# Expert weights in 4 MB loads of 32 KB per partition, and a new order at the end of the expert stage

## What is computed

```python
logits = h @ router_w + router_b
top_logit, top_e = lax.top_k(logits, 4)            # 4 of 32 experts for each token
gate = jnp.minimum(xe @ w_gate[e] + b_gate[e], 7.0)
up = jnp.clip(xe @ w_up[e] + b_up[e], -7.0, 7.0)
act = (up + 1) * (gate * jax.nn.sigmoid(1.702 * gate))
y = act @ w_down[e] + b_down[e]                     # times the token's weight, summed over its experts
```

## Time and profile before

| | |
|---|---|
| median of the runs | 1764.72 us |
| the profiled execution's own time | 1764.61 us |
| its span, first to last instruction | 1762.8 us |
| PE busy | 1638.9 us, 93% |
| DVE busy | 731.0 us, 41% |
| ACT busy | 283.2 us, 16% |
| granted PE clock, mean | 0.992 of full speed |
| moved by DMA | 537.21 MB |
| mean DMA rate | 305 GB/s |

### The profile page before, as it was taken

One profiled execution on the slowest core, in us unless ns is written; L12 is line 12 of the kernel. 1 busy time (PEld: TensorE's weight loads), 2 busy tenths in 40 slices (PEclk: granted clock), 3 DMA queues, 4 the chain that ended last, 5 costly groups with the idle time before them and its releaser, 6 DMA issues.

```text
span 1762.8 us, 19011 instructions
## 1 busy us (share of the span) xinstructions
PE 1638.9 (93%) x7248; PEld 887.6 (50%) x7248; DVE 731.0 (41%) x1325; ACT 283.2 (16%) x623; POOL 25.2 (1%) x30
## 2 busy tenths in 40 slices
PE   5999999999999798898997988998999999999998
PEld 3466686534333242332332423332686878888743
DVE  3785532332324223233142232332234663777755
ACT  3123450301010010100100101000243334010000
POOL 0110000000000000000000000000000000000000
PEclk9999999999999999999999999999999999999999
DMA  9895235899999999999999999999624333444440
GB/s 381 299 332 163 96 111 204 342 430 429 431 430 429 430 430 430 429 430 430 430 429 430 429 430 430 430 429 418 220 96 143 129 111 144 143 173 162 153 181 24
DMA packets 86255, 537.21 MB, mean 305 GB/s; under 512 B 6160, under 2 KB 7568, under 8 KB 59952
## 3 DMA queue, kind: packets, MB, share of 16 engines
q1 hardware_dynamic: 82384, 530.60, 74.2%
q10 hardware_dynamic: 3808, 5.78, 0.9%
HBM read 535.31 MB, written 1.05 MB: 304 GB/s over the span
## 4 chain that ended last, share of the span: by engine, by line
PE 69%; DMA 24%; DVE 4%; DVEq 1%; issue 1%; ACT 1%; POOL 0%; ACTq 0%; SPq 0%
PE ps L1953 22%; PE ps L2332 22%; DMA ring<-in_w_up 12%; DMA ring<-in_w_gate 10%; PE ps L2678 6%; PE ps L2872 5%; PE ps L2308 3%; PE ps L2393 2%; DMA arena<-in_w_down 2%; PE ps L2783 1%; DVE arena L1163 1%; DMA const<-in_const 1%; PE ps L2189 1%; PE ps L1965 1%; PE ps L2372 0%
## 5 line engine op out<-in xcount | busy, mean ns | idle before, releaser
L2332 PE MATMUL ps<-ring,arena 128*64 128x512 f32 x2288 | 513.8, 597 | 54.0 <-DMA ring<-in_w_gate 21.0
L2332 PEld LDWEIGHTS ps<-ring,arena 128*64 128x64 f32 x2288 | 161.2, 137 | 388.0 <-issue 316.7
L1953 PE MATMUL ps<-arena,ring 128*128 128x256 f32 x896 | 199.9, 381 | 0.3 <-ACT arena L790 0.3
L2332 PE MATMUL ps<-arena 128*64 128x512 f32 x784 | 177.8, 598 | 12.1 <-DMA arena<-in_w_up 5.7
L1953 PEld LDWEIGHTS ps<-arena,ring 128*128 128x128 f32 x896 | 168.4, 190 | 33.2 <-issue 6.8
L1953 PE MATMUL ps<-ring,arena 128*128 128x512 f32 (+1 forms) x480 | 164.0, 496 | 1.5 <-ACT arena L907 1.3
L862 ACT ACTIVATE arena<-ps 128x512 f32<-128x512 f32 x32 | 19.1, 598 | 670.4 <-PE ps L2372 670.4
L1953 PEld LDWEIGHTS ps<-ring,arena 128*128 128x128 f32 x480 | 90.8, 191 | 65.0 <-issue 56.9
L2332 PEld LDWEIGHTS ps<-arena 128*64 128x64 f32 x784 | 55.5, 138 | 120.2 <-issue 103.6
L1448 DVE TENSOR_TENSOR arena<-ps,arena 128x512 f32<-128x512 f32 x32 | 22.1, 692 | 201.2 <-PE ps L2332 201.2
L1473 DVE TENSOR_TENSOR arena<-ps,g_moe 64x512 f32<-64x512 f32 x32 | 21.9, 684 | 189.5 <-PE ps L2332 189.5
(11 more groups left out here) (351 smaller groups left out, 1558.5 us busy)
## 6 DMA issues: line engine op xcount, KB each, us to landing
ring<-in_w_up SPq DMA_DIRECT2D x54, 2048.0 KB, 33.8
ring<-in_w_down SPq DMA_DIRECT2D x54, 2048.0 KB, 32.2
ring<-in_w_gate SPq DMA_DIRECT2D x47, 2048.0 KB, 33.6
ring<-in_w_in SPq DMA_DIRECT2D x23, 2048.0 KB, 8.1
arena<-in_w_down SPq DMA_DIRECT2D x17, 2048.0 KB, 32.0
arena<-in_w_up SPq DMA_DIRECT2D x16, 2048.0 KB, 31.3
arena<-in_w_gate SPq DMA_DIRECT2D x15, 2048.0 KB, 30.8
ring<-in_w_ada SPq DMA_DIRECT2D x12, 2048.0 KB, 17.1
```

Of the source, the lines that this page charges most:

```text
L1953: last = pe.matmul(dst, a, b, start=k == 0, stop=k == len(terms) - 1)
L2332: mm = pe.matmul(dst[CAP * g:CAP * g + CAP, :], stationary(half, c), w[:, c, 512 * g:512 * g + 512], start=half == 0 and c == 0, stop=half ...
```

## The change

A matrix is read eight rows to a partition: partition p holds rows 8p to 8p + 7, 32 KB in one piece, in one load of 4 MB into two adjacent slots (slots 5 and 6 are now in `arena`). Such a load waits until both slots are free, and PE waits for it before the first half. This holds from block 18 of the first group to block 19 of the last, 170 blocks in 85 loads. Blocks 0 to 17 of the first group, down 2 and down 3 of the last come as halves of 2 MB (four of a partition's eight rows, 16 KB), and the last half in four loads, one matrix row of each partition (4 KB) at a time. The first blocks go out in the order 4, 6, 7, 5, 8.

Feature 8p + c now stands on partition p. The gate and up products take as moving operand, for each half of the bank, groups of four columns out of every eight (`by_rows`), so that what follows keeps its layout. The biases are loaded in whole rows and put in that order by two copies on POOL, whose buffer lies where `hperm` is written later, so ACT waits for them before its first copy. The shift comes by eight matmuls of 64 columns for each of n = 6 and n = 7. The first gather waits for all four copies to `hperm`.

In the last group the branch comes after gate 3 and the turn of expert 2's activation. Behind it stand up 3, all four rows of the first combine, down 2, the turn of expert 3's activation, down 3, and the second combine, whose first row waits for the first half of `y_out` alone.

```diff
-        hperm = area(1024, 2048).rearrange("p (t h c d) -> p t h c d", t=TT, h=2, c=4)
+        hperm = area(1024, 2048).rearrange("p (t j d) -> p t j d", t=TT, j=KC)
+        btab_in = area(1024, 2048)
...
+        PAIRED = 18
...
+        def moe_area(s, slots=1):
+
+            r = moe_ring(s)
+            return area(13312 + SLOT * (s - 5), SLOT * slots) if r is None else ring[:, r * SLOT:(r + slots) * SLOT]
+
+        def moe_block(k):
+            a = area(7680, SLOT) if k == ASIDE else moe_area(moe_place(k) % MRING)
+            return a.rearrange("p (c n) -> p c n", c=4)
+
+        def moe_pair(k):
+            return moe_area(moe_place(k) % MRING, 2)
+
         def moe_ring(s):
 
-            return None if s in (4, 5) else (W_MOE + (s if s < 4 else s - 2)) % RING
-
-        def moe_block(k):
-            if k == ASIDE:
-                return area(7680, SLOT).rearrange("p (c n) -> p c n", c=4)
-            s = moe_place(k) % MRING
-            r = moe_ring(s)
-            a = ring[:, r * SLOT:(r + 1) * SLOT] if r is not None else area(13312 + SLOT * (s - 4), SLOT)
-            return a.rearrange("p (c n) -> p c n", c=4)
+            return None if s in (5, 6) else (W_MOE + (s if s < 5 else s - 2)) % RING
...
+        PAIRED_AT = (1, 3, 5, 7)
+        LAST_BLOCK = N_EXP * BLK_EXP - 1
+        HALF_LOADS = [k for k in range(PAIRED) if k != ASIDE] + [LAST_BLOCK - 2, LAST_BLOCK]
+        LAST_HALVES = ((EG - 2, 2), (EG - 1, 2))
...
+            def matrix(g, q, m):
+                return t[("w_gate", "w_up", "w_down")[m]][bass.ds(g * EG + q, 1), :, :].rearrange(
+                    "e (p c) n -> p (e c) n", c=KC)
+
             def block_load(X, g, q, m, half, k):
-                src = t[("w_gate", "w_up", "w_down")[m]][bass.ds(g * EG + q, 1), half * 512:half * 512 + 512, :]
-                sp_.dma_start(moe_block(k).rearrange("p c n -> p (c n)"),
-                              src.rearrange("e (p c) n -> p (e c n)", c=4)).then_inc(moe_loaded(k), 16)
-
-            def expert_load(X, u, g, q, m, last=False):
+                sp_.dma_start(moe_block(k), matrix(g, q, m)[:, 4 * half:4 * half + 4, :]).then_inc(moe_loaded(k), 16)
+
+            def expert_load(X, u, g, q, m, last, start):
 
                 k = weight_block(q, m, last)
-                for half in range(2):
-                    sp_.wait_ge(X["used"], u * GROUP_BLOCKS + (X["before"] - MRING + k + half + 1))
-                    block_load(X, g, q, m, half, k + half)
-
-            def group_loads(X, u, g, last, done=0):
...
+                order = {4: (1, 0), 6: (1, 1), 8: (0, 2), 10: (2, 0), 12: (2, 1)}
+                for n in (4, 6, 7, 5, 8, 9, 10, 11, 12, 13) if first else range(4, 14):
+                    (q, m), half = order[n - n % 2], n % 2
+                    if not first:
+                        sp_.wait_ge(X["used"], u * GROUP_BLOCKS + (X["before"] - MRING + n + 1))
+                    elif n == 6:
+                        sp_.wait_ge(sem("merged_done"), 4)
+                    elif n in (4, 5, 8):
+                        sp_.wait_ge(X["used"], W_MOE - RING + {4: 4, 5: 5, 8: 6}[n])
...
+            pool.wait_ge(sem("bias_in"), 64)
+            for g in range(2):
+                rows = slice(64 * g, 64 * g + 64)
+                pool.tensor_copy(btab[rows].rearrange("p (m f c) -> p m f c", m=2, c=4),
+                                 btab_in[rows].rearrange("p (m f g c) -> p g m f c", m=2, g=2, c=4)[:, g]
+                                 ).then_inc(sem("bias_in"), 1)
+                pool.drain()
...
+                if i == 0:
+                    act.wait_ge(sem("bias_in"), 66)
                 act.wait_ge(sem("hp_tr"), i + 1)
-                act.activation(hperm[:, i // 2, i % 2].rearrange("p c d -> p (c d)"), bank(4 + i), ACT.Copy,
+                act.activation(hperm[:, i // 2].rearrange("p j (h d) -> p h j d", h=2)[:, i % 2],
+                               bank(4 + i).rearrange("p (j d) -> p j d", j=KC), ACT.Copy,
...
-                dve.tensor_tensor(y[r0:r0 + CAP, 0:512], bank(2)[0:CAP, :], g_moe[0:CAP, 0:512], ALU.mult)
+                first = dve.tensor_tensor(y[r0:r0 + CAP, 0:512], bank(2)[0:CAP, :], g_moe[0:CAP, 0:512], ALU.mult)
+                if last and q == EG - 1:
+                    first.then_inc(last_scaled, 1)
...
+                if n == 6:
+                    for j in range(KC):
+                        last = pe.matmul(bank(mod_bank(n))[0:64, j:j + 1], src[:, j:512:KC], cst(C_ROW0, 1), start=True, stop=True)
+                else:
+                    for q in range(4):
+                        last = pe.transpose(bank(mod_bank(n))[:, P * q:P * q + P], src[:, P * q:P * q + P], ident)
...
+                if n == 7:
+                    for j in range(KC):
+                        last = pe.matmul(dst[64:128, j:j + 1], src[:, j:512:KC], one, start=True, stop=True)
+                        if j == 0:
+                            tell_used(last)
...
-                b = bank(4 + 2 * tt + half).rearrange("p (c j d) -> p j d c", c=4, j=4)
+                b = bank(4 + 2 * tt + half).rearrange("p (j c d) -> p c d j", j=KC, c=4)
...
+                    halved = (start is not None and b < PAIRED) or (last and (q, m) in LAST_HALVES)
+                    by_row = last and (q, m, half) == (EG - 1, 2, 1)
+                    if by_row:
+                        pass
+                    elif b == ASIDE or moe_slot(b) in PAIRED_AT:
+                        pe.wait_ge(moe_loaded(b), u * (16 * GROUP_BLOCKS // MRING) + 16 * moe_loads(b))
+                    elif halved:
+                        n, per_pass = half_loads(b if b < PAIRED else LAST_BLOCK - 2)
+                        pe.wait_ge(moe_loaded(b), (passed if last else start) * (16 * per_pass) + 16 * n)
...
+                    by_rows = w.rearrange("p c (f g a) -> p c g f a", g=2, a=4)
                     for c in range(4):
+                        if by_row and c < 3:
+                            pe.wait_ge(row_in(c), number * 16 + 32)
+                        elif by_row:
+                            n, per_pass = half_loads(LAST_BLOCK)
+                            pe.wait_ge(moe_loaded(b), passed * (16 * per_pass) + 16 * n)
                         if between and (half, c) == (0, 2):
                             between[0]()
                         for g in range(2):
+                            moving = w[:, c, 512 * g:512 * g + 512] if m == 2 else by_rows[:, c, g]
                             mm = pe.matmul(dst[CAP * g:CAP * g + CAP, :], stationary(half, c),
-                                           w[:, c, 512 * g:512 * g + 512], start=half == 0 and c == 0,
...
+            def first_gate(X, it, u, first, start):
 
                 pe.wait_ge(X["s4_ready"], it + 1)
                 if first:
-                    pe.wait_ge(sem("hp_read"), 3)
+                    pe.wait_ge(sem("hp_read"), 4)
                 gather_round(X, it, 0)
                 gather_round(X, it, 1)
-                if first:
-                    pe.wait_ge(sem("hp_read"), 4)
...
-                if not last:
-                    gate(X, it, u, EG)
+                if last:
+                    pe.wait_ge(X["y_read"], it * EG + 3)
+                    pe.wait_ge(X["comb_read"], it * 8 + 1)
+                    return
+                up(X, it, u, 3, start)
+                gather(X, it + 1)
+                down(X, it, u, 2, start=start)
+                gate(X, it, u, EG, start)
                 act_transpose(X, it, 3)
-                if last:
-                    combine(X, it, 0, 2)
-                else:
-                    combine(X, it, 0)
-                    down(X, it, u, 3)
-                    up(X, it, u, EG)
-                    combine(X, it, 1)
-
-            def last_expert(X, u):
-
-                down(X, u, u, EG - 1, True)
-                for r in (2, 3):
+                combine(X, it, 0)
+                down(X, it, u, 3, start=start)
+                up(X, it, u, EG, start)
+                combine(X, it, 1)
+
+            def last_expert(X, u, passed, number):
+
+                up(X, u, u, 3)
+                for r in range(4):
                     combine_row(X, 0, r, LAST_BANKS[0][r])
+                down(X, u, u, 2, True, passed=passed)
+                act_transpose(X, u, 3)
+                down(X, u, u, EG - 1, True, passed=passed, number=number)
+                pe.wait_ge(last_scaled, number + 4)
+                combine_row(X, 1, 0, LAST_BANKS[1][0])
                 pe.wait_ge(X["y_read"], u * EG + (EG + 1))
-                for r in range(4):
+                for r in range(1, 4):
                     combine_row(X, 1, r, LAST_BANKS[1][r])
```

More of the change, by code:

```diff
@@ L2316, in gather, with halves @@
                     gather_round(X, it, r)
[L2318 removed]
+            def halves(X, u, q, m, dst, stationary, last=False, between=None, start=None, passed=None,
+                       number=None):
                 for half in range(2):
```

176 lines of the change are left out of this document (90 added, 86 removed).

## The result

The changed kernel takes **1770.49 us** (median of 8 runs, 1768.61 to 1776.90), against 1764.26 for the kernel before (8 runs, 1762.51 to 1768.64) beside it. The ratio is **1.0035, 95% interval 1.0026 to 1.0044**: slower by a third of a per cent, clear of the interval, where 1760.0 was forecast, and above the forecast's range. The profiled execution was the longest of the eight (1776.9, span 1775.1). The same kernel run again later gave 1770.19, so a second profile of it (*again*, 1770.09, span 1768.3) stands beside the first.

A forecast was written before the change was run, and what follows sets the result against it. Transfers were taken to set the end from about 340 us until the last weights land, PE before 320 us and after. Terms -6.6 + 0.6 + 1.3 + 0.1 = -4.6 gave 1760.0 us, range (8 in 10) 1755 to 1767.5.

The forecast's parts named there:

- The larger pieces: First term, expert weight stream: 85 loads of 4 MB save 680 packets an engine at 9.7 ns each, -6.6 us.
- two-point fit: Weight stream: 16,384-byte packets at 430 GB/s and 2,048-byte ones at 387 give 9.7 ns a packet beside its bytes.
- Rival 1: Weight stream: completions and seams between halves cost nothing any more, -8.0 in all, 1756.6 us; 15%.
- rival 2: Weight stream: larger pieces save nothing, 1766.6 us (8%), or a third of the forecast saving, 1764.4 us (8%).
- Before the experts: Shift products ahead of the experts: 16 half-width instructions take 1.92 us; nothing for n = 7, +1.3 us for n = 6.
- rival 4: Expert stream: longer idle pieces of PE lower its clock, some +50 us, 1,815 us; 4%.
- The end: Last group: pairing up 3 leaves PE idle, less branch and combine rows off the last stretch; +0.6 us, between -1 and +2.
- laying: Last group: new order laid on the old landing times, from gate 3's pair at 1204.8 to the end at 1238.0 us.
- The grain in the stream: Expert stream: a pair is asked for 3.5 us later, hidden by the DMA queue; 0 us.
- strided moving operand: Gate and up products reading 4 of every 8 columns: no charge taken, upper bound double.
- rival 3: Gate and up products: moving operand read slower, some 2,100 us at double, some 1,875 at half as much more; 5%.
- rival 5: Expert stream: reads 32 KB apart collide in memory, 387 GB/s, 1,859 us; 4%.

The follow-up runs named there:

- blocks2: Changed kernel with every expert matrix in two loads of 2 MB, each waited for by itself; 1770.75 us, ratio 1.0033 to the kernel before.
- wide: Changed kernel with the one-column shift products of the sixth and seventh part written 64 columns wide; 1767.08 us, ratio 1.0010 to the kernel before.
- order: Kernel before with only the change's new order of PE's last work, its 2 MB loads kept; 1764.73 us, ratio 1.0001.
- tail: Changed kernel with gate 3 and up 3 of the last group loaded and waited for in halves; 1765.82 us, ratio 0.9997 to the kernel before.
- branch: Changed kernel with PE's branch into the last steps moved ahead of gate 3 of the last group; 1768.64 us, ratio 1.0025 to the kernel before.
- keeper: Changed kernel with three 128-column transposes added ahead of the sixth part's one-column products; 1770.81 us, ratio 1.0039 to the kernel before.
- narrow: Kernel before with extra one-column products put in for the sixth and seventh part, into columns that are overwritten; 1776.39 us, ratio 1.0077.
- best: Changed kernel with the edits of tail and wide, its branch left where the change has it; 1763.18 us, ratio 0.9995 to the kernel before.
- both: Changed kernel with the edits of ends and wide together; 1762.60 us, ratio 0.9988 to the kernel before.
- shift: Changed kernel with the sixth and seventh part turned by the old instructions; values land on wrong partitions, more expert passes run; 2713.86 us.
- ends: Changed kernel with the edits of tail and branch together; 1765.97 us, ratio 1.0007 to the kernel before.

## Why the prediction was wrong

The sign of the first term was right, and two terms of the sum failed, each by about 4 us in the same direction. Both left out the same thing: what the granted clock does behind a run of narrow products or a wait.

**The larger pieces, -6.6: right in sign, a fifth too large.** blocks2 against after gives 5.2 us, 5.2 / 680 = 7.6 ns a packet instead of 9.7, if all of it is put down to the packets; loads and their small packets were halved with them, and no run parts these. The two-point fit took the whole difference between 387 and 430 GB/s for overhead of packets. The Trainium skill's 3 cycles ("DMA: Bandwidth & Descriptors") would have made it 2.4, an estimate from the page's figure; the measurement is twice that. Rival 1's -8.0 is out by its size, and so are both forms of rival 2.

**Before the experts, n = 6 and 7, +1.3: the step that failed most.** "Now there are 16 instructions of half as many columns. By half of 0.24 each they take 1.92": the 16 took 2.08, twice, which makes +1.6, and the stretch with its other instructions came to +2.05 in wide. What was missing is what they do to the clock: 32 of them, nearly in a row, with one moving column each, and the granted clock falls to 0.50 for the product behind. Wide puts this at 3.1 us of the kernel's time, *again*'s timeline at 2.4. Together 4.5 to 5.2 for 1.3, at the upper bound that I had set for another reason (0.24 each). I asked what the instructions cost and not what TensorE would be granted after them; rival 4 had the clock only in the stream.

**The end, +0.6: wrong by about 4.** Order shows no cost of the new order (+0.1 us, with an interval of -1.4 to +1.8); tail shows that pairs there cost 4.4 by the medians (3.0 by the marks of the two profiles). Two of the laying's steps fail. "Gate 3 starts only with its whole pair, 1197.7 + 7.1 = 1204.8; turn 0.6; the branch (1.76 of idle before) ends by 1207.1, under the wait for up 3's pair at 1207.5": gate 3 took 8.78 us at the lower clock after its 3.17 us wait (in the other profile, after 2.44), and the branch 2.39 and 2.49 us, so that up 3 started 11.8 us after gate 3 instead of 9.8, 2.2 us behind its landing. Where gate 3 ran at the full clock (branch, wide, keeper) the branch was under the wait, as laid out, and up 3 ran at the lower clock instead. What the laying lacked above all is this 1.7 us, one product at the lower clock behind a long wait or the branch. From there my laying held: 30.82 us from up 3 to the first turn for 30.5, down 3 behind 1.09 us of idle time and 0.65 of turn for 1.5, no wait on the rows. From gate 3 to that turn: 42.58 for 40.3, 2.3 lost. The rest lies ahead of gate 3: its pair is there only 3.1 us earlier against the first expert product than the second half was before (869.91 for 873.03), not the 5 that the rate gives. Blocks2 takes this apart. With the change's layout and loads of 2 MB gate 3's second half starts at 874.46 us after that product: pairs are worth 4.5 us against it, and all else in the change costs 1.4 against before (0.9 and 1.7 against order and narrow, where it is 873.55 and 872.80). One place shows it: from 20 to 30 us behind the first expert product DMA moves 406 GB/s in before and 392 and 407 in order and narrow, but 351 to 382 in the eleven profiles with the change's layout, blocks2's 370 among them. The order and the waits of the first loads were changed there; no run took them back, so the cause of the 1.4 is not shown.

**What held.** The grain in the stream costs nothing: PE's longest wait for weights is 2.6 us for 1.3, two in one as rival 4 had it, and PE has its 45 us to spare. The 32 matmuls of a gate or up product take 7.09 us as before: the strided moving operand costs nothing here, rival 3 is out. 433 GB/s: rival 5 is out. The first gather waits 0.50 us for the fourth copy in *again*, where 0.32 were for DVE: +0.2 for +0.1.

**The ledger.** -5.2 (rate) + 5.2 (shift, 2.05 of its own and 3.1 of clock) + 4.5 (end) + 0.2 = +4.7. Measured: +4.6 in *again*, +6.2 at first. That the sum meets the first of these so closely is partly luck. By the marks *again* divides otherwise: +5.5 to the first expert product, -3.1 from there to gate 3 (-4.5 for the pairs, +1.4 of the unexplained), +3.0 from gate 3 to the turn, where +0.6 was forecast. Backward, tail and wide together should win 7.5. *best* won 7.0 by the medians and 5.6 when each is taken against its own kernel before. Against before, it should then stand at -2.8, and stands at -1.0. What its profile shows of the rest are the 1.4 us ahead of gate 3 and the 1.7 of down 1 at the lower clock; together they are large enough, but no run took either out.

**Rival 4** was right in its mechanism and wrong in its place. In the stream the clock of 0.97 costs nothing; at the end the same fall costs 1.4 to 1.7 us each time. These are the idle times of PE ahead of gate 3 or up 3 in the last group (of down 3 in before), and the product behind, in all profiles whose product ran without a wait inside: 1.16, 1.30, 1.76 and 1.85 us: 7.09 each. 2.05: 8.79. 2.13, 2.19, 2.38, 2.39: 7.09, but for one 7.21. 2.44, 2.49, 2.58, 2.71, 2.72, 2.78, 2.99, 3.17: 8.47 to 8.79. The length of the idle time alone does not decide it: down 1 of the last group, behind 1.98 or 1.99 us, took 8.78 in all five profiles that have such a wait (branch, both, best, wide, keeper), less idle than the four at 7.09 to 7.21. The Trainium skill ("TensorE: Matmul & The Clock Gate", on the oscillation in real kernels) describes it: short products between longer waits for DMA meet the lower clock each time. These rows agree in direction, with waits shorter than the page's 3 to 5 us, though the six waits of up to 2.8 us in the stream before stand beside a granted clock of 0.99.

## What to carry to other kernels

Price an instruction on TensorE by what it does to the granted clock as well: a run of one-column products cost at least as much through the wide product behind it (2.4 to 3.1 us) as by itself (2.05), and writing the same products 64 columns wide took the former back at no price. Larger transfers pay in the stream and cost where it ends: load the last matrices there in smaller units, which PE can start on earlier, and lay out each wait there with the clock of the product behind it. Before trusting a gain in one stage, cut the profile at marks and see whether that stage got shorter.

## What was not expected of the hardware

- Sixteen products of 128x64 by one column and four transposes, then sixteen more, leave the granted clock at 0.50 for the next 5 us (110 to 115 us in *again*); eight of 128x128 by one column in before do not (1.00, shift). At 64 columns each they take 2.13 us for 2.08 and leave it at 1.00.
- Loads of 4 MB in packets of 32 KB go at 432 to 433 GB/s where loads of 2 MB in packets of 16 KB go at 430: 7.6 ns a packet, if it is all the packet's.
- The branch into another part of PE's program, with the register waits around it, costs 2.05 to 2.78 us of idle time where it is uncovered, in eight profiles (1.76 and 1.73 at its old place, before and narrow). The Trainium skill ("Advanced Engine Details and Errata", control flow timing) gives about 0.1 us for a compare and branch. The trace has no row for these alone, so it does not test the figure; the step as a whole costs some twenty times as much.
- The clock also falls or stays with no change of the code ahead of it: the twelve transposes of the turn back took 1.51 us before, in shift, wide and ends, 2.68 to 2.80 in the other profiles, order's among them, whose code is before's there.
